# Moving the late modulation dots from the GDN heads to the first expert down stage

## The reference, cut to what matters

```python
def adaln_params(cvec, w, b):
    m = jax.nn.silu(cvec) @ w + b
    return [mi[..., None, :] for mi in jnp.split(m, ADA_CHUNKS, axis=-1)]

for i in range(DEPTH):
    sh1, sc1, g1, sh2, sc2, g2 = adaln_params(c, ada_w[i], ada_b[i])
    csh1, csc1, cg1, csh2, csc2, cg2 = adaln_params(c_ctx, ada_w[i], ada_b[i])
    h = modulate(x, norm1_g[i], sh1, sc1)
    # layer 0: gated delta rule mixer; layer 1: window attention
    # then the expert layer: rmsnorm, modulate(sh2, sc2), peer_ffn, times g2, added to x
```

## Time and profile before

| | |
|---|---|
| median of 3 runs (lowest, highest) | 3908.66 us (3891.73, 3910.57) |
| the profiled execution | 3908.66 us, its span 3907.4 us |
| busy over the span | PE 3501.7, DVE 2998.5, ACT 1597.9, POOL 1429.4 us |
| GDN heads | 340 to 735 us |
| first expert down stage | 1791 to 2350 us |

### The profile page before, as it was taken

One profiled execution on the slowest core, in us unless ns is written; L12 is line 12 of the kernel. 1 busy time (PEld: TensorE's weight loads), 2 busy tenths in 40 slices (PEclk: granted clock), 3 DMA queues, 4 the chain that ended last, 5 costly groups with the idle time before them and its releaser, 6 DMA issues.

```text
span 3907.4 us, 61132 instructions
## 1 busy us (share of the span) xinstructions
PE 3501.7 (90%) x24101; PEld 3246.8 (83%) x24101; DVE 2998.5 (77%) x6196; ACT 1597.9 (41%) x2472; POOL 1429.4 (37%) x796
## 2 busy tenths in 40 slices
PE   7998888999987777778999998999999999988899
PEld 5667888889976666677999997799998999977799
DVE  3796777448999999995878886788773877766575
ACT  2323444333323333332333334555664333447453
POOL 1335444234774444444545540077666000000000
PEclk8999999899999999999999999999999999998899
DMA  5332113224865666668889972167777788642255
GB/s 189 105 134 69 53 59 106 79 91 120 277 190 192 222 219 218 218 226 323 328 315 339 347 280 87 39 182 217 252 258 270 254 280 274 235 136 81 92 173 162
DMA packets 250829, 751.28 MB, mean 192 GB/s; under 512 B 24112, under 2 KB 101808, under 8 KB 243248
## 3 DMA queue, kind: packets, MB, share of 16 engines
q1 hardware_dynamic: 124288, 431.28, 34.4%
q10 hardware_dynamic: 89392, 181.86, 13.1%
q0 software_dynamic: 36864, 134.23, 9.1%
HBM read 661.82 MB, written 84.93 MB: 191 GB/s over the span
## 4 chain that ended last, share of the span: by engine, by line
PE 58%; DVE 28%; DMA 6%; ACT 4%; issue 2%; POOL 1%; ACTq 0%; SPq 0%; DVEq 0%
PE ps L139 57%; DVE paone L88 11%; DVE n_sq L114 3%; DMA paGg<-paG 2%; DVE g_b L81 2%; DMA ring<-in_v 2%; DVE lo L81 2%; ACT hi L134 1%; DVE n_rs L114 1%; DVE paone L87 1%; PE ps L142 1%; DVE paR L81 1%; POOL lo L81 1%; DVE cond L114 1%; DMA ring<-in_gdn_in 1%
## 5 line engine op out<-in xcount | busy, mean ns | idle before, releaser
L81 POOL TENSOR_TENSOR lo<-ring,hi 128x1024 fp32r<-128x1024 f32 x392 | 966.8, 2472 | 1279.7 <-ACT hi L134 1279.3
L134 ACT ACTIVATE hi<-ring 128x1024 fp32r<-128x1024 f32 x725 | 768.5, 1061 | 918.2 <-PE ps L139 629.0
L81 DVE TENSOR_TENSOR lo<-ring,hi 128x1024 fp32r<-128x1024 f32 (+1 forms) x333 | 406.4, 1222 | 237.4 <-ACT hi L134 236.8
L139 PE MATMUL ps<-pahh,hi 128*128 128x384 f32 (+1 forms) x1152 | 421.5, 366 | 25.3 <-POOL lo L81 22.4
L88 DVE TENSOR_SCALAR paone<-paR 128x128 bf16<-128x128 bf16 x1152 | 441.5, 449 | 0.0
L139 PE MATMUL ps<-pahl,hi 128*128 128x384 f32 (+1 forms) x1152 | 409.6, 356 | 0.0
L139 PE MATMUL ps<-pahh,lo 128*128 128x384 f32 (+1 forms) x1152 | 408.9, 355 | 0.0
L139 PE MATMUL ps<-pchh,hi 128*128 128x256 f32 x1152 | 333.8, 290 | 12.8 <-POOL lo L81 11.0
L139 PE MATMUL ps<-pchl,hi 128*128 128x256 f32 x1152 | 326.3, 283 | 0.0
L139 PE MATMUL ps<-pchh,lo 128*128 128x256 f32 x1152 | 325.9, 283 | 0.0
L139 PEld LDWEIGHTS ps<-pahh,hi 128*128 128x128 f32 x1152 | 230.1, 200 | 32.9 <-POOL lo L81 25.1
(11 more groups left out here) (474 smaller groups left out, 9811.6 us busy)
## 6 DMA issues: line engine op xcount, KB each, us to landing
ring<-in_u SPq DMA_DIRECT2D x256, 512.0 KB
ring<-in_v SPq DMA_DIRECT2D x256, 512.0 KB
ring<-in_adat SPq DMA_DIRECT2D x80, 512.0 KB, 3.5
paA<-paga ACTq DMA_DIRECT2D x128, 192.0 KB
paG<-paR ACTq DMA_DIRECT2D x12, 2048.0 KB, 8.5
paAg<-paA ACTq DMA_DIRECT2D x16, 1536.0 KB, 7.8
paGg<-paG ACTq DMA_DIRECT2D x16, 1536.0 KB, 21.7
ring<-in_ffn_up SPq DMA_DIRECT2D x44, 512.0 KB
```

The lines of the kernel that those rows point to most:

```text
L81: return Op(self.e.tensor_tensor(out, a, b, op) if self.real else None)
L134: return Op(self.e.activation(out, a, ACT.Copy, scale=scale) if self.real else None)
L139: return Op(self.e.matmul(out, l, r, start=start, stop=stop, skip_group_check=skip) if self.real else None)
```

## The change

The 56 late tiles are taken out of the ring's stream. `ada_late` gets buffers of its own: three tiles `late_w`, the conditioning rows and the columns of sums; the unused product of a dot goes to `n_sq`. It returns two functions, which `first_down` calls once in each of its 128 iterations: `load(i)` on ScalarE issues the load of tile i / 2 in even iterations below 112 (behind a wait for the dot three tiles back), and `dot(i)` on VectorE reduces tile (i - 4) / 2 in even iterations from 4 to 114, after the row sum of the iteration. The conditioning rows are loaded at iteration 0 and go through SiLU at iteration 3; biases and scales follow at iteration 118. In `gdn_heads` the dots, the load of the rows and their SiLU are gone. (`peer` and `peer_down` get the same two calls behind a flag that nobody sets.)

```diff
--- before.py
+++ after.py
@@ plan
-    for k in range(24, 80):
-        out.append((("adat", k), d["adat"][k], 1024, True))
@@ gdn_heads
-            rows_loaded, rows_ready, dot = ada_late(st)
-            dots_at = {12: 2, 14: 2, 18: 2, 21: 1, 24: 1, 27: 1, 30: 1}
...
-                        if engine is vector:
-                            for _ in range(dots_at.get(n, 0)):
-                                dot()
...
@@ first_down, scalar(), after the high halves of iteration i
+                late[0](i)
@@ first_down, vector(), after the row sums of iteration i
+                late[1](i)
@@ ada_late
+        row = alloc(st, "late_row", [128, 2, 1024])
+        tiles = [alloc(st, f"late_w{i}", [128, 1024]) for i in range(3)]
+        rest = [x.bitcast(BF16) for x in n_sq]
...
+        def load(i):
+            if i == 0:
+                act.dma(row[:, :, :], d["crow"]).then_inc(s_row, 0, 16)
+            if i == 3:
+                act.wait_ge(s_row, 0)
+                act.act(row[:, :, :], row[:, :, :], ACT.Silu).then_inc(s_silu, 0)
+            if i % 2 == 0 and i < 112:
+                k = i // 2
+                if k >= 3:
+                    act.wait_ge(s_dot, used[k - 3][-1])
+                act.dma(tiles[k % 3][:, :], d["adat"][24 + k]).then_inc(s_load[k % 3], k, 16)
+
+        def dot(i):
+            if i % 2 == 0 and 4 <= i < 116:
+                k = (i - 4) // 2
+                if k == 0:
+                    dve.wait_ge(s_silu, 0)
+                dve.wait_ge(s_load[k % 3], k)
+                for j, col in enumerate(used[k]):
+                    if col >= 2:
+                        dve.wait_ge(s_dot, col - 2)
+                    dve.dot(rest[col % 2], tiles[k % 3][:, :], row[:, j, :], dots[:, col:col + 1]).then_inc(s_dot, col)
```

More of the change, by code:

```diff
@@ L1102, in eg @@
                     act.act(qd[:, dr], v4(ps[dr]), ACT.Exp).then_inc(s_copy, (hd, "eG", dr))
-                for n in range(5):
-                    if hd == 0 and n == 0:
-                        rows_loaded()
-                    if hd == 0 and n == 3:
-                        rows_ready()
+                for _ in range(5):
                     yield True
@@ L1435, in peer_first @@
             first_up(name, h, A, G, R, one, ga, groups, sparse, gather, dot)
-            first_down(name, Ag, Gg, av, ga, halves, groups, sparse, gather, add)
+            first_down(name, Ag, Gg, av, ga, halves, groups, sparse, gather, add, ada_late(st))
     def sparse_rows(sparse):
@@ L1878, in first_up, with first_down @@
         vector()
-    def first_down(name, Ag, Gg, av, ga, halves, groups, sparse, gather, add):
+    def first_down(name, Ag, Gg, av, ga, halves, groups, sparse, gather, add, late):
         s_gated, s_high, s_act, s_res = S("expert_gated"), S("expert_high"), S("expert_act"), S("expert_added")
@@ L2000, in first_down, with peer @@
         rest()
-    def peer(l, a, z, name, then):
+    def peer(l, a, z, name, then, late=False):
         w = z - a
@@ L2026, in peer @@
             peer_up(l, nt, name, h, A, G, R, one, ga, groups)
-            peer_down(l, nt, name, Ag, Gg, av, halves, groups, then)
+            peer_down(l, nt, name, Ag, Gg, av, halves, groups, then, ada_late(st) if late else None)
     def peer_groups(name, A, G, Ag, Gg):
@@ L2355, in peer_up, with peer_down @@
         vector()
-    def peer_down(l, nt, name, Ag, Gg, av, halves, groups, then):
+    def peer_down(l, nt, name, Ag, Gg, av, halves, groups, then, late):
         s_act, s_res = S("expert_act"), S("expert_added")
@@ L2395, in scalar @@
                 hi_to(v[i])
+                if late:
+                    late[0](i)
                 k = i // 8
@@ L2449, in ada_late @@
     def ada_late(st):
+        s_load = [S(f"late_loaded{i}") for i in range(3)]
         s_row, s_silu, s_dot = S("late_cond_loaded"), S("late_cond"), S("late_dot")
-        row = mem.over("late_row", [128, 3, 2, 1024], "hi")[:, 2]
-        junk = n_rs[:, :].bitcast(BF16)
+        row = alloc(st, "late_row", [128, 2, 1024])
+        tiles = [alloc(st, f"late_w{i}", [128, 1024]) for i in range(3)]
+        rest = [x.bitcast(BF16) for x in n_sq]
         dots = alloc(st, "late_dots", [128, 80])
-        parts = [(k, j) for k in range(56) for j in range(2 if k < 24 else 1)]
-        left = list(enumerate(parts))
+        used, c = [], 0
         for k in range(56):
-            release[at[("adat", 24 + k)]] = (s_dot, (k, 1 if k < 24 else 0))
-        def rows_loaded():
-            act.dma(row, d["crow"]).then_inc(s_row, 0, 16)
-        def rows_ready():
-            act.wait_ge(s_row, 0)
-            act.act(row, row, ACT.Silu).then_inc(s_silu, 0)
-        def dot():
-            if not left:
-                dve.wait_ge(s_dot, (55, 0))
+            n = 2 if k < 24 else 1
+            used.append(range(c, c + n))
+            c += n
+        def load(i):
[19 more added lines that the diff above has]
+                    dve.dot(rest[col % 2], tiles[k % 3][:, :], row[:, j, :], dots[:, col:col + 1]).then_inc(s_dot, col)
+            if i == 118:
+                dve.wait_ge(s_dot, 79)
                 dve.tt(mod[:, 0, 40:48, :], dots[:, 0:16].rearrange("p (m j) -> p m j", j=2),
@@ L2476, in dot @@
                 ada_scale(1, 1, "late", (0,))
-                return
-            col, (k, j) = left.pop(0)
-            i = at[("adat", 24 + k)]
-            if col == 0:
-                dve.wait_ge(s_silu, 0)
-            else:
-                dve.wait_ge(s_dot, parts[col - 1])
-            dve.wait_ge(arrived[slot(i)], i)
-            dve.dot(junk, slots[slot(i)], row[:, j, :], dots[:, col:col + 1]).then_inc(s_dot, (k, j))
-        return rows_loaded, rows_ready, dot
+        return load, dot
     def swa():
```

## The result

The kernel got slower by what the sum had said. Its median is 3940.28 us (3918.5 to 3947.09, 9 runs), that of before 3908.66 us (3891.73 to 3919.99, 9 runs); the ratio is 1.0075 with a 95% interval of 1.0053 to 1.0097, so +31.6 us by the medians. The profiled execution took 3935.16 us, its span is 3933.8 us. Single executions of one kernel lie up to 29 us apart, so a whole-kernel time that stands on one execution is rough.

A forecast was written before the change was run, and what follows sets the result against it. TensorE was taken to bound both stages, idling in the heads mostly behind VectorE. Heads -31 us and down stage +62 us (56 + 8 + 2 + 1 - 5) gave 3908.66 + 31 = 3940 us, 8-in-10 range 3900 to 3982.

The forecast's parts named there:

- The heads, -31 us: GDN heads: removing late dots, the rows' load with SiLU and small end operations saves 27 + 3 + 1 = 31 us.
- -27 for the dots: Eight GDN heads: without the late dots TensorE idles 3.4 us less for a head, 27 us in all; likely 15 to 40.
- -3 -1 for the rows and the end: Heads' start: 3 us won without the rows' load and SiLU; heads' end: 1 us for VectorE's six small modulation operations.
- half gone: One head's 1.06 us TensorE gap behind VectorE: shrinks by 0.5 us, since the exponentials it needs end late too.
- VectorE's room, +56 us: Down stage: late dots exceed VectorE's 0.79 us free of 8.60 us a pair, as VectorE and GpSimd exclude each other; 56 us.
- 41 + 15: Down stage: two-dot pairs, 1.71 us over in 24 pairs, 41 us; one-dot pairs, 0.46 us over in 32 pairs, 15 us.
- The gates' waits, -5 us: Down stage: VectorE's 15.0 us of waits for the gates shrink in the slower rhythm, giving TensorE back 5 us.
- The DMA side and ScalarE's queue, +8 and +2 us: Down stage: added late-tile traffic costs 8 us; late tiles behind the gates on ScalarE's queue cost 2 us, ends 0 and 20.
- dots cost nothing: Second rival, down stage: VectorE and GpSimd overlap, two-dot pairs take 7.91 us, only DMA's 10 us remains; 3888 us, chance 0.09.
- nothing given back: Fourth rival, heads: they stay as long, since another engine is late at each gap; 3967 us, chance 0.05.
- the draw: Third rival: the heads give 40 + 4 us and the down stage costs 45; 3910 us, chance 0.12.
- The first rival: Down stage: DMA engines and ScalarE's queue become the limit, another 30 us over 14 groups; 3970 us, chance 0.14.

The follow-up runs named there:

- b_short: Kernel before, with the 80 late dots in the heads cut from 1024 to 8 columns, loads kept; 3885.11 us, beside 3904.28 us of before.
- a_pool8: Kernel after, with GpSimd making the low half of odd weight tiles for 8 of 1024 columns; down stage 564.9 us, profiled run 3863.18 us.
- b_dve: Kernel before, with the low halves of all down-stage weight tiles on VectorE, none on GpSimd; 3945.25 us, ratio to before 1.0091.
- a_three: Kernel after, all dots whole, but only the first three late tiles loaded and reused; down stage 601.1 us, profiled run 3904.84 us.
- a_short: Kernel after, with the late dots in the down stage cut to 8 columns, all 56 loads kept; down stage 620.7 us, profiled run 3935.59 us.
- a_dve: Kernel after, with the low halves of all down-stage weight tiles on VectorE, none on GpSimd; 3932.03 us, ratio to before 1.0068.

## Why the prediction was right, and where it was lucky

**The heads, -31 us.** Right in size, and in reason for the larger part. Predicted -27 for the dots and -3 -1 for the rows and the end; measured -28.0 (b_short) and -4.2, by the heads' own length. The gap behind the state's copy is gone and ScalarE's share is unchanged, as was said. But all of it was to be idle time, and about 7 of the 32.2 us are clock, 5.1 of them behind gaps of 1.8 to 2.0 us; that stood in no term. Idle time gave 25 us and not 31. The gaps were laid out wrongly, too. The one of 1.06 us, "half gone", is 0.98 or 1.37 us now, in either kind of head. The one of 1.86 us stood in three heads of eight, behind 6.2 us of waits in all, and not in every head. The rest came from gaps of 1.77 and 2.03 us in the other heads, which the single head of the earlier trace rows doesn't show. That the total came out is in part luck.

**VectorE's room, +56 us.** The mechanism held: both inputs of a late dot in SBUF, exclusion with GpSimd, TensorE waits for the factor's low half. The Trainium skill, "SBUF — State Buffer", section "Who interferes with whom", has the lock hold for a whole instruction whoever comes first; the trace agrees, with dots of up to 3.42 us and GpSimd's tile at 3.18. The size was too high: +1.29 us for a pair with two dots (9.89 - 8.60), not +1.71, since a dot costs 1.14 us and the exclusion 2.19 us; and about +0.25 us for one dot (249.0 - 242.1 = 6.9 us over 28 pairs of groups 7 to 13), not +0.46. And the 8.60 us that it is counted from are not TensorE's own rhythm: without GpSimd's tile a pair takes 8.32 us (a_pool8, b_dve), so the stretched low half cost 0.28 us in each pair already. The terms 41 + 15 are nearer 31 + 8, and the stage with the dots alone is +32.7 us, with the gates' waits gone.

**The gates' waits, -5 us.** Right in direction: VectorE's 15.0 us became 1.1 us, and the fourth group, 42.0 us before, is 40.1 us beside 39.5 and 39.6. What TensorE got back by it no run shows apart; in the kernel before its one long gap there was 4.60 us, with 3.4 us of clock behind it.

**The DMA side and ScalarE's queue, +8 and +2 us.** This is the step that failed in size: the loads cost 27.6 us on top of the dots. It was named under what the change adds ("ScalarE may also be held at the issue while the queue is full"), and the upper end of 20 us for the queue alone was nearer than the 2 us taken. I had priced bandwidth, by which a group needs 37.8 us, and a_pool8 does the same traffic in 35.0 us. What costs is the load right behind the gates together with GpSimd's tile: a hold of up to 7.88 us, then a low half stretched by 1.83 us, a gap of 2.2 to 3.5 us in a group of one-dot pairs, and behind five of these seven 1.7 us of half clock. The same holds without GpSimd's tile left the stage at 564.9 us (a_pool8). That the clock falls behind a gap stood in no term. Why the transfers come late, on ScalarE's queue as a held issue and on SyncE's as late gates, stays open.

**The sum.** +62 predicted, +60.3 measured, but as 33 (dots) + 28 (loads on top of them), where I had 51 + 11. Two errors of some 17 us cancelled. Counted the other way round it is 52 (loads) + 8 (dots on top of them), further still from the prediction. That the total is right shows nothing of its parts; only a_three and a_short do. Of the rivals, "dots cost nothing" falls (32.7 us), "nothing given back" falls (-32.2 us), and the draw falls with 60.3 us where it had 45. The first rival is half right: the queue matters, the DMA engines are not the limit (a_pool8), and its price came in place of a part of mine and not on top.

## What to carry to other kernels

Before work is moved to a stage with "free" VectorE time, add up by starts what VectorE and GpSimd do one after the other there, not the busy share. A stage whose engine seems busy throughout can still hide a short wait in every round; compare its rhythm with a run that lacks the suspect. A load that is issued by a computing engine should not stand right behind a large one in small pieces on the same queue, but here neither another queue nor another order won the time back: both moved the wait to the gates. Issuing the gates earlier was not tried. What stands behind a held issue counts as much as the hold: one of 7.7 us cost a gap of 1.84 us without GpSimd's tile and 3.25 us with it. And price a gap of TensorE with the clock behind it, which also counts in the stage that gets shorter: in the down stage of the kernel after, seven gaps of eleven between 1.96 and 3.45 us cost another 1.7 us each.

## What the runs showed of the hardware

- An issue on ScalarE's queue behind 1.5 MB in pieces of 1 KB holds the engine up to 7.88 us (after), 9.84 (a_short) and 11.32 us (a_dve), at a median of 0.335 us. What TensorE loses is less: holds of 6.6 to 7.9 us left gaps of 1.7 to 3.5 us (after), holds of 5.8 to 7.7 us gaps of 0 to 1.85 us (a_pool8).
- TensorE's granted clock was 0.51 in the 2 us behind a gap of 3.45 us, and 1.00 through pairs with a gap of 1.3 us each. The length of the gap doesn't decide it alone: gaps of 3.13 and 2.95 us (after) and 2.5 us (a_three) left it at 1.00, gaps of 1.77 us (heads, before) and 1.84 us (a_pool8) were followed by 0.5.
- The exclusion isn't simply the two durations added: GpSimd's tile of 2.40 us, begun during a dot, cost VectorE 2.19 us. With the tile moved to VectorE (b_dve) or cut to 8 columns (a_pool8) an undisturbed pair of 48 matmuls took 8.32 us, with it 8.60 us (before).
- The DMA engines carried 365 GB/s at a share of 0.96 over 525 us (a_pool8). In the kernel after, whose engines were held up, the same loads ran at 347 GB/s and 0.92 between 1800 and 2350 us.
